# Decay tree on GpSimd, weight splits and the z projection moved inside a scan over heads, residuals read before the next split

## The chip, the cores and the metric

The kernel runs on 1 core of one Trainium2 chip. The metric is device time in microseconds. Three runs of the kernel before gave 2747.86 us as their median (2746.51 to 2750.76). The engines are called PE (TensorE, matrix products), DVE (VectorE), ACT (ScalarE), POOL (GpSimd) and SP (SyncE, which here only issues DMAs). Each runs its own instructions in order, and they meet through semaphores.

## The reference

Two blocks run one after the other on 512 tokens of width 1024, in float32. All products are float32-exact in effect, which the kernel reaches by splitting each operand into a high and a low part.

```
# first block, layer 0: gated linear recurrence (16 heads of 128, two directions, 256 context + 512 tokens)
p = (rms_norm(x) * (1 + scale) + shift) @ w_in          # five streams a head: q, f forward, f backward, v, z
q = silu(p[0]);  f = lb + (1 - lb) * sigmoid(p[1:3]);  k = 1 - f;  g = log(f)
S_t = diag(exp g_t) S_{t-1} + k_t v_t^T;   o_t = S_t^T q_t       # both directions, summed
y = rms_norm(o) * g_norm * silu(z);   x = x + gate * (y @ w_out)
# layer 1: 2-D Fourier mixer on 8 groups, then rms_norm(x, final_g)
# second block: 16 meta tokens in front, then
h = h + 0.5 * swiglu_ffn(rmsnorm(h))      # d_ff 2816
h = h + token_mixer(rmsnorm(h))           # causal convolutions, RG-LRU, gates
h = h + 0.5 * swiglu_ffn(rmsnorm(h));  out = rmsnorm(h)[16:]
```

## The kernel before

**Weights.** All weights come as one stream of 376 blocks of 128x1024 (512 KB), in two slots. For a block in slot `s`, SP loads `w_raw`; ACT copies it to `w_hi` (a rounded copy, `cut`, L812) once PE is done with the block that was in this slot; DVE computes `w_lo = w_raw - w_hi` (its own `cut`, L1265), which frees `w_raw` for the next load and releases PE. PE then runs three products for each 128x128 tile (`three`, L409): high by high, high by low, low by high. `after(k)` on ACT and DVE is the cut of block k+2, and on ACT it first waits until PE is done with block k. Where DVE or ACT has the cut in its queue decides what stands behind it.

**Heads.** Six blocks belong to one head: q, two f streams, v, z and a block for the modulation of a later layer. PE's loop (`pe_head(j + 1, j)`, 15 passes, one head in front and one behind outside the loop) projects head i = j+1 and between its parts does the scan of head j. Projections k go to PSUM bank `a = k % 2` (tokens) and bank `2 + k % 2` (context); ACT's `stage(k)` cuts a block, then reads the banks (`q_st`, `f_st`, `v_st`, `z_st`) and counts `acc_free` up, and PE's `free(k)` waits on that counter. The last two stages are z (k = 4) and the modulation (k = 5). After z is read, DVE's `prepare` makes `f_st`, `K`, `Q` and `ksum` of the new head and signals `gates_ready`. The banks 4 to 7 belong to the scan.

**The scan of a head** uses a tree of decays with 7 levels. At level l DVE's `merge(l)` does, in order: the product of neighbours `tree(l + 1)` from `tree(l)` (L1461; the leaves are `f_st`), growing `K` by the sibling's decay (L1469, then `k_grown`), growing `Q` (L1469), and placing PE's last scores into `ST` by a mask (L1446). ACT's `weave(l)` copies `K` into `K_now` (L932), and PE's `level(l)` multiplies `K_now` by `Q` (L568) once `weave(l)` and the growing of `Q` in `merge(l - 1)` are done. Then PE turns `K` (L581), makes the outer products (L590), DVE passes the states along (`passed`, L1487 and L1493), PE makes the output in bank 7 (L600 to L602), ACT squares it (`osq`, L937), PE sums the squares (`norm`, L609), ACT takes the root (`rt`, L942), and a head later DVE inverts it (L1504).

DVE's order in a head is: cut for stage 0, merges 0 to 2, cut for stage 1, merges 3 to 5, cut for stage 2, merge 6, the inversion, the states, the modulation, cut for stage 4, `prepare`, cut for stage 5. ACT's order at the end of a head is `stage(4)` (cut, `z_st`), square of the output, `stage(5)`, root. GpSimd issues DMAs only: in a loop over the heads it waits on `gate_used` and loads `gate_raw`, then `x1`, the Fourier tables, `meta` and at the end the output.

**Residuals.** `residual` and `raw_residual` add a finished product (nb blocks, PSUM) to a row of the stream. For each row m, DVE does all cuts of the nb blocks, then waits for the product, adds it (`stt`, L1592 or L1693), and where a norm follows, adds up the squares that ACT makes (L1303, L1308, or L1726 and L1727). The sums feed a matmul with `ones_d` (L445, L448) and a root on ACT.

**The first feed-forward** starts with unnormed rows and applies the rate afterwards. A pair of blocks (`one`: gate, up) ends in one row of `hid`. After the first pair PE also makes the mean for the final norm of the first block (L739). ACT has the root for it, `root(NFIN, ...)`, ahead of all pairs of the feed-forward; DVE inverts it in the second pair and applies it in the third and fourth.

Of the kernel before, what the change touches and what calls it, by code (L numbers as in the profile page):

```python
# [27 lines left out]
ALU = mybir.AluOpType  # L28
ACT = mybir.ActivationFunctionType
ds = bass.ds  # L30
# [20 lines left out]
RW = 4  # L51
EARLY = 4
EPS = 1e-6
LEVELS = 7
# [17 lines left out]

PER = {"head": 25 + 2 * (KD - 1), "mix": 74}

# [84 lines left out]
def program(nc, wts, ada_in, gate_in, x_in, ctx_in, meta_in, vec_in, mask_in, ident_in, dft_in, chan_in, out):  # L159
    nblocks = wts.shape[0]  # L160
    with ExitStack() as top:
# [135 lines left out]
        gates_ready = sem("gates_ready")  # L297
        k_grown, k_woven = sem("k_grown"), sem("k_woven")
        y_ready, y_hi_ready = sem("y_ready"), sem("y_hi_ready")
# [33 lines left out]
        def row(t, j):  # L333

            return t[:, j] if isinstance(j, int) else t[:, ds(j, 1)].rearrange("p a n -> p (a n)")

        def rate(j):
# [42 lines left out]
        @block.gpsimd  # L380
        def _(pool):
            pool.dma_start(xc[:], ctx_in).then_inc(xc_in_s, 16)
            pool.dma_start(masks[:], mask_in).then_inc(const_in_s, 16)
            pool.dma_start(ident[:], ident_in).then_inc(ident_in_s, 16)
            with pool.Fori(0, HEADS) as i:
                pool.wait_ge(gate_used, i + 1)
                pool.dma_start(gate_raw[:], gate_in[ds(i, 1)].rearrange("a p n -> p (a n)")
                               ).then_inc(gate_loaded, 16)
# [13 lines left out]
        def _(pe):  # L402
# [86 lines left out]
            def pe_head(i, j):  # L489
                def free(k):  # L490
                    pe.wait_ge(acc_free, i * 6 + (k + 1))

# [309 lines left out]
        def _(act):  # L802
# [70 lines left out]
            def act_head(i, j, f):  # L873
# [5 lines left out]

                def stage(k):  # L880

                    if i is None:
                        if j is not None and k < EARLY:
                            after(k)
                        return
                    if k == 3:
# [5 lines left out]
                    a, c = ps[:, k % 2], ps[:, 2 + k % 2]  # L892
# [226 lines left out]

            def feed_forward(tags, last_R, n, last, gated, product, hi):  # L1120
                c0 = TM - n
                for tag, count in zip(tags, FF_GROUPS):
                    S, before = ffn[tag]
                    with act.Fori(0, count) as i:
                        st.enter(i, 2)
                        after(0)
                        act.wait_ge(S["scaled"], i + (before + 2))
                        run(gated[:, 0:n], gated[:, 0:n], ACT.Silu).then_inc(S["gate"], 1)
                        after(1)
                        act.wait_ge(S["product"], i + (before + 1))  # L1130
                        run(row(hi, i)[:, c0:TM], product[:, 0:n], ACT.Copy).then_inc(S["hi"], 1)
                    st.leave(count)
                    final = tag == tags[-1]
# [3 lines left out]

            feed_forward(("f1a", "f1b", "f1c"), RD1, TM, False, sg1, hid1, hid1_hi)
            block_norm(NMIX)
# [107 lines left out]
            root(NF2, ps[:, 6], rate2[:, 0:T])  # L1247
            feed_forward(("f2a", "f2b", "f2c"), RD2, T, True, sg, hid, hid_hi)
            fetch_root()
# [5 lines left out]
        def _(dve):  # L1255
# [131 lines left out]

            def tree(l):

                if l == 0:  # L1390
                    return f_st[:]
                at = TA - (TA >> (l - 1))
                return f_tree[:, :, at:at + (TA >> l)]

            def dve_head(i, j, f):
# [57 lines left out]
                def merge(l):  # L1453


                    n = 2 ** l
                    prev = tree(l).rearrange("p d (m h) -> p d m h", h=2)
# [4 lines left out]
                    if l == 0:  # L1462
                        place(LEVELS, 4)
                    own.wait()

# [5 lines left out]
                    dve.wait_ge(k_woven, j * LEVELS + (l + 1))  # L1471
                    grow(K, 0, TA, 0).then_inc(k_grown, 1)
                    pe((3, 4, 6, 7, 8, 9, 10)[l])
                    if l:
# [5 lines left out]
                def passed(g_):  # L1480

                    pe((12, 14, 16)[g_])
                    whole_tile = tree(LEVELS)
                    acc = ps[:, 4 + g_ % 2].rearrange("p (x c) -> p x c", c=P)
# [37 lines left out]
                if j is None:  # L1522
# [54 lines left out]
            def residual(R, trips, nb, out_row, factor, n, sums, N=None, ahead=True, done=0):  # L1577
# [35 lines left out]
            for k in range(EARLY):  # L1613
                after(k)
                st.wait_done(dve, k)
                stt(x1[:, k], ps[:, k], gates[:, k, 0:1], x1[:, k], ALU.mult, ALU.add).then_inc(RC["res"], 1)
                add_square(RC, k, *sums)
            st.leave(1)
# [64 lines left out]
            def raw_residual(R, N, trips, nb, src, factor, gain, hi, lo, add):  # L1683


                with dve.Fori(0, trips) as i:
                    st.enter(i, 2 * nb)
                    for a in range(2):
                        for q in range(nb):
# [3 lines left out]
                        stt(src(m_), ps[:, 2 * a], factor(m_), src(m_), ALU.mult, ALU.add).then_inc(R["res"], 1)  # L1693
                        dve.wait_ge(N["hi"], m_ + 1)
                        stt(lo(m_), src(m_), gain(m_), hi(m_).bitcast(F32), ALU.mult, ALU.subtract
# [409 lines left out]
```

## Time and profile before

| | us |
|---|---|
| median of 3 runs | 2747.86 |
| lowest and highest | 2746.51 and 2750.76 |
| the profiled execution | 2748.82 |
| its span | 2747.2 |
| PE busy | 2564.4 (93% of the span) |
| DVE busy | 1625.9 (59%) |
| ACT busy | 1027.7 (37%) |
| POOL busy | 13.1 (28 DMA instructions) |
| mean granted clock of PE | 0.977 |

The span is that of the hardware profiler; the time of the execution also holds what lies around it. The heads take from about 55 to 997 us of the span, the Fourier mixer to 1350, its output product to 1447, the first feed-forward to 1842, the token mixer to 2352, the second feed-forward to the end.

In a timeline a row is: start in us from the span's start, length in us, engine, line, operation, output<-inputs, shape, count; the bracket at the end is the engine's idle time before it and what ended it. PE's records overlap each other (a 128x512 matmul is recorded at 0.40 us and the next one starts 0.23 us later), and so do DVE's by about 0.1 us, so distances between starts tell more than lengths. In a table of windows the columns are: the window, its length, then for PE, PEld, DVE, ACT and POOL the busy time and the count of instructions, then the granted clock of PE, the share of the DMA engines and GB/s. In a view by lines a row is: line, engine, operation, tiles, shapes, count, then busy us, mean ns of one, and idle time before them.

### The profile page before, as it was taken

To read this page: it belongs to the slowest core of one execution; us is meant where nothing else is said; L and a number is where in the kernel's file an instruction comes from. 1 tells how busy PE (TensorE), PEld (TensorE's weight loads), DVE (VectorE), ACT (ScalarE), POOL (GpSimd) and SP (SyncE) were. 2 spreads that over 40 slices of the span, in tenths; PEclk is the share of its full clock that TensorE was granted. 3 is DMA by queue.
4 is the path that set the end of the run, shared out by engine and by line. 5 is a ranking of instruction groups with operands and counts; after the bars stand their busy time and mean duration, and the time that the engine had idled before them with its cause. 6 is when DMAs were issued, how large, how long until landed. Compare 5 with 4: busy or idle time off the path is not lost.

```text
span 2747.2 us, 40135 instructions
## 1 busy us (share of the span) xinstructions
PE 2564.4 (93%) x14516; PEld 2191.1 (80%) x14516; DVE 1625.9 (59%) x2388; ACT 1027.7 (37%) x1349; POOL 13.1 (0%) x28
## 2 busy tenths in 40 slices
PE   6999999999999988999899999989999889999996
PEld 2788888888888775888688999988888757788885
DVE  5567777777777754333345443457999855534445
ACT  3334443444344323333234322235455533542222
POOL 0000000000000000000000000000000000000000
PEclk9999999999999998999899999999999999999998
DMA  5212211121112222222122222222222212222232
GB/s 219 69 62 76 70 61 61 62 83 61 61 53 89 79 85 69 69 69 69 45 94 74 91 87 92 92 92 85 89 87 91 85 54 88 89 99 92 92 99 84
DMA packets 59817, 224.34 MB, mean 82 GB/s; under 512 B 6496, under 2 KB 6496, under 8 KB 59136
## 3 DMA queue, kind: packets, MB, share of 16 engines
q1 hardware_dynamic: 56544, 207.94, 22.3%
q0 software_dynamic: 3232, 15.86, 1.5%
q8 instruction: 25, 0.41, 0.1%
q14 instruction: 16, 0.13, 0.0%
HBM read 221.68 MB, written 2.10 MB: 81 GB/s over the span
## 4 chain that ended last, share of the span: by engine, by line
PE 79%; DVE 9%; ACT 5%; issue 5%; DMA 1%; DVEq 0%; ACTq 0%; SPq 0%; POOL 0%
PE ps L409 71%; PE ps L568 3%; ACT w_hi L812 2%; PE ps L590 1%; DVE K L1469 1%; PE ps L466 1%; DVE w_lo L1265 1%; DVE cv L1826 1%; ACT K_now L932 1%; PE ps L581 1%; ACT L910 1%; DVE f_tree L1461 1%; DMA ada_raw<-in_ada_weights_dram 1%; PE ps L609 1%; DVE n_tmp L1826 0%
## 5 line engine op out<-in xcount | busy, mean ns | idle before, releaser
L1265 DVE TENSOR_TENSOR w_lo<-w_raw,w_hi 128x1024 fp32r<-128x1024 f32 x360 | 440.2, 1223 | 618.2 <-ACT w_hi L812 616.4
L812 ACT ACTIVATE w_hi<-w_raw 128x1024 fp32r<-128x1024 f32 x360 | 381.2, 1059 | 973.3 <-PE ps L409 939.5
L409 PE MATMUL ps<-n_hi,w_hi 128*128 128x512 f32 (+1 forms) x992 | 323.8, 358 | 29.7 <-DVE w_lo L1265 15.4
L409 PE MATMUL ps<-n_lo,w_hi 128*128 128x512 f32 (+1 forms) x992 | 320.2, 355 | 0.0
L409 PE MATMUL ps<-n_hi,w_lo 128*128 128x512 f32 (+1 forms) x992 | 319.8, 354 | 0.0
L409 PE MATMUL ps<-h_hi,w_hi 128*128 128x512 f32 x640 | 273.0, 427 | 9.2 <-DVE h_lo L1292 4.6
L409 PE MATMUL ps<-h_hi,w_lo 128*128 128x512 f32 x640 | 255.0, 398 | 0.0
L409 PE MATMUL ps<-h_lo,w_hi 128*128 128x512 f32 x640 | 254.8, 398 | 0.0
L409 PEld LDWEIGHTS ps<-n_hi,w_hi 128*128 128x128 f32 x992 | 175.4, 191 | 65.9 <-issue 20.2
L409 PEld LDWEIGHTS ps<-n_lo,w_hi 128*128 128x128 f32 x992 | 176.0, 190 | 26.7 <-issue 0.2
L409 PEld LDWEIGHTS ps<-n_hi,w_lo 128*128 128x128 f32 x992 | 175.8, 190 | 26.6
L568 PE MATMUL ps<-Q,K_now 128*128 128x128 f32 x896 | 129.4, 288 | 27.3 <-ACT K_now L932 25.8
L409 PEld LDWEIGHTS ps<-h_hi,w_hi 128*128 128x128 f32 x640 | 121.7, 190 | 39.3 <-issue 8.1
L568 PEld LDWEIGHTS ps<-Q,K_now 128*128 128x128 f32 x896 | 117.1, 191 | 44.3 <-ACT K_now L932 38.1
L409 PE MATMUL ps<-xg_hi,w_hi 128*128 128x264 f32 x704 | 144.8, 287 | 4.5 <-DVE w_lo L1265 4.5
L409 PEld LDWEIGHTS ps<-h_hi,w_lo 128*128 128x128 f32 x640 | 121.5, 190 | 29.2
L409 PE MATMUL ps<-xg_lo,w_hi 128*128 128x264 f32 x704 | 143.9, 287 | 0.0
L409 PE MATMUL ps<-xg_hi,w_lo 128*128 128x264 f32 x704 | 143.0, 284 | 0.0
L409 PEld LDWEIGHTS ps<-h_lo,w_hi 128*128 128x128 f32 x640 | 122.1, 191 | 24.2 <-issue 2.2
L409 PE MATMUL ps<-hid_hi,w_hi 128*128 128x264 f32 (+1 forms) x528 | 141.1, 321 | 0.0
L409 PE MATMUL ps<-hid_lo,w_hi 128*128 128x264 f32 (+1 forms) x528 | 141.0, 322 | 0.0
L409 PE MATMUL ps<-hid_hi,w_lo 128*128 128x264 f32 (+1 forms) x528 | 140.6, 320 | 0.0
(327 smaller groups left out, 5012.9 us busy)
## 6 DMA issues: line engine op xcount, KB each, us to landing
w_raw<-in_weights_dram SPq DMA_DIRECT2D x376, 512.0 KB, 3.3
ada_raw<-in_ada_weights_dram SPq DMA_DIRECT2D x4, 2048.0 KB, 25.2
gate_raw<-in_gate_weights_dram POOLq DMA_DIRECT2D x16, 512.0 KB, 4.8
x<-in_x_dram SPq DMA_DIRECT2D x1, 2048.0 KB, 9.3
x<-in_x_dram POOLq DMA_DIRECT2D x1, 2048.0 KB, 11.1
out_dram<-fin POOLq DMA_DIRECT2D x1, 2048.0 KB, 6.5
xc<-in_ctx_dram POOLq DMA_DIRECT2D x1, 1024.0 KB, 10.7
F_raw<-in_seq_dft_dram POOLq DMA_DIRECT2D x1, 1024.0 KB, 5.5
```

The costliest lines, as they stand in the source:

```text
L409: last = nc.tensor.matmul(o, w, xp, start=start and n == 0, stop=stop and n == 2)
L466: last = nc.tensor.matmul(ps[0:2, n], csil[:, k], raw_[:, :, k * P:(k + 1) * P], start=k == 0, stop=k == KD - 1)
L568: last = nc.tensor.matmul(ps[:, 5 - l % 2, tile(t)], K_now[:, l % 2, tile(t)], woven(Q, t * P, P, 2 ** l, 1), start=True, stop=True)
L581: last = nc.tensor.transpose(ps[:, 6, tile(x)], K[:, d, tile(ORDER[d][n])], ident[:])
L590: last = nc.tensor.matmul(ps[:, 4 + g_ % 2, tile(x)], KT[:, x], V[:, ORDER[d][n]], start=True, stop=True)
L609: nc.tensor.matmul(ps[:, 5], ones_h[:], osq[:], start=True, stop=True).then_inc(pe_scan, 1)
L812: run(w_hi[:, s], w_raw[:, s], ACT.Copy).then_inc(hi_ready[s], 1)
L910: run(z_st[:], a, ACT.Silu).then_inc(acc_free, 1)
L932: run(K_now[:, l % 2], woven(K, TC, T, 2 ** l, 0), ACT.Copy).then_inc(k_woven, 1)
L1265: tt(w_lo[:, s], w_raw[:, s], w_hi[:, s].bitcast(F32), ALU.subtract).then_inc(lo_ready[s], 1)
L1461: own.mark(tt(tree(l + 1), prev[:, :, :, 0], prev[:, :, :, 1], ALU.mult))
L1469: return tt(both(t, size, n, half), both(t, size, n, half), paired(*by, n), ALU.mult)
```

## The change

- The products of the decay tree leave DVE's `merge` and run on GpSimd, all seven of a head in a row after `gates_ready`, each waiting on the one before through a new semaphore `tree_grown`. GpSimd's load of `gate_raw` for the next head follows them. DVE's merges 1 to 6 and the passing of the states wait on `tree_grown`, and ACT waits for the first product before it writes `f_st` again.
- In a head's DVE order the cut for stage 0 moves behind merge 1, that for stage 1 behind merge 4, that for stage 2 behind merge 6. In `merge(0)` the placing of the diagonal goes behind the growing of `K`.
- z goes to PSUM bank 2 instead of bank 0, and projection 0 of the next head no longer waits for `z_st`. ACT cuts the block of stage 4, then squares the output, then reads z.
- In residuals the product is read right after it is done, ahead of the last cut instead of behind it.
- ACT takes the root of the final norm after the first pair of the first feed-forward.

```
+            pool.wait_ge(gate_used, 1)
+            pool.dma_start(gate_raw[:], gate_in[0:1]...).then_inc(gate_loaded, 16)
+            with pool.Fori(0, HEADS - 1) as i:
+                pool.wait_ge(gates_ready, i + 1)
+                for l in range(LEVELS):
+                    if l:
+                        pool.wait_ge(tree_grown, i * LEVELS + l)
+                    pair = siblings(l)
+                    nc.gpsimd.tensor_tensor(tree(l + 1), pair[:, :, :, 0], pair[:, :, :, 1], ALU.mult
+                                            ).then_inc(tree_grown, 1)
+                pool.wait_ge(gate_used, i + 2)
+                pool.dma_start(gate_raw[:], gate_in[ds(i + 1, 1)]...).then_inc(gate_loaded, 16)
...
     (PE)
-                    pe.wait_ge(acc_free, i * 6 + (k + 1))
+                    pe.wait_ge(acc_free, i * 6 + (k + (1 if k else 0)))
-                    a, c = k % 2, 2 + k % 2
+                    a, c = Z_BANK if k == 4 else k % 2, 2 + k % 2
...
     (ACT, a head)
                     elif k < 3:
                         if j is not None:
                             dve(1)
+                            act.wait_ge(tree_grown, j * LEVELS + 1)
...
                 cut_output()
+                refill(4)
+                squares_of_output()
                 stage(4)
-                squares_of_output()
                 stage(5)
...
     (DVE, a head)
-                    own.mark(tt(tree(l + 1), prev[:, :, :, 0], prev[:, :, :, 1], ALU.mult))
-                    if l == 0:
-                        place(LEVELS, 4)
-                    own.wait()
+                    else:
+                        dve.wait_ge(tree_grown, j * LEVELS + l)
...
                     grow(K, 0, TA, 0).then_inc(k_grown, 1)
+                    if l == 0:
+                        place(LEVELS, 4)
+                    own.wait()
...
-                next_block(0)
                 merge(0)
                 merge(1)
+                next_block(0)
                 merge(2)
-                next_block(1)
                 merge(3)
                 merge(4)
+                next_block(1)
                 merge(5)
+                merge(6)
                 next_block(2)
-                merge(6)
...
     (DVE, residual; raw_residual and the first four rows alike)
-                        for q in range(nb):
+                        for q in range(nb - 1):
                             if cuts:
                                 after(a * nb + q)
                         st.wait_done(dve, a * nb + nb - 1)
...
                         stt(r_, acc, factor(m_), r_, ALU.mult, ALU.add).then_inc(R["res"], 1)
+                        if cuts:
+                            after(a * nb + nb - 1)
                         if sums:
                             add_square(R, m_, *sums)
...
     (ACT, feed-forward)
-            root(NFIN, ps[:, 4], n1["sq"][:, 0])
+                    early = 0 if before else 1
+                    if early:
+                        one(S, 0, 0, 0)
+                        st.leave(1)
+                        aside()
...
+            feed_forward(("f1a", "f1b", "f1c"), RD1, TM, False, sg1, hid1, hid1_hi,
+                         lambda: root(NFIN, ps[:, 4], n1["sq"][:, 0]))
```

## Rows read from the trace of the kernel before

**Rows 1.** Windows: one pass of the heads' loop; the stretch after the third block's wait.

```profile
603.67:659.13 55.46, 53.02 (x323) 45.94 (x323) 40.71 (x70) 23.20 (x34) 0.53 (x1) 1.00 0.20 66
...
1461.50:1466.50 5.00, 4.99 (x23) 4.99 (x24) 3.05 (x4) 2.08 (x3) 0.00 (x0) 0.51 0.51 162
```

**Rows 2.** Timeline of PE, one pass of the heads' loop.

```profile
492.76 1.13 PE L609 MATMUL ps<-osq,ones_h 128*128 128x512 f32 x2 [0.66 <-ACT osq L937]
...
504.53 0.40 PE L409 MATMUL ps<-h_hi,w_lo 128*128 128x512 f32 x1
505.83 1.23 PE L568 MATMUL ps<-Q,K_now 128*128 128x128 f32 x8 [0.90 <-ACT K_now L932]
...
509.91 1.05 PE L568 MATMUL ps<-Q,K_now 128*128 128x128 f32 x8
...
518.28 1.16 PE L568 MATMUL ps<-Q,K_now 128*128 128x128 f32 x8 [0.79 <-ACT K_now L932]
...
529.28 0.40 PE L409 MATMUL ps<-h_hi,w_lo 128*128 128x512 f32 x1
529.77 0.65 PE L581 MATMUL ps<-ident,K 128*128 128x128 f32 x4
```

**Rows 3.** Timeline of DVE, the same pass.

```profile
492.59 1.27 DVE L1436 TENSOR_SCALAR f_st<-f_st,lbt 128x768 f32<-128x768 f32 x2 [0.47 <-ACT z_st L910]
...
495.91 0.68 DVE L1442 TENSOR_TENSOR ksum<-K 128x512 f32<-128x512 f32 x1
...
501.20 1.23 DVE L1265 TENSOR_TENSOR w_lo<-w_raw,w_hi 128x1024 fp32r<-128x1024 f32 x1 [3.47 <-ACT w_hi L812]
...
504.10 0.96 DVE L1469 TENSOR_TENSOR K<-K,f_st 128x768 f32<-128x768 f32 x1
...
528.68 0.96 DVE L1469 TENSOR_TENSOR K<-K,f_tree 128x768 f32<-128x768 f32 x1
```

**Rows 4.** Timeline of ACT, the same pass.

```profile
490.32 1.28 ACT L910 ACT_TABLE_LOAD   x1
491.62 0.60 ACT L910 ACTIVATE z_st<-ps 128x512 f32<-128x512 f32 x1
492.11 0.59 ACT L937 ACTIVATE osq<-ps 128x512 f32<-128x512 f32 x1
...
502.48 0.60 ACT L896 ACTIVATE q_st<-ps 128x512 f32<-128x512 f32 x1
...
516.79 0.38 ACT L901 ACTIVATE f_st<-ps 128x256 f32<-128x256 f32 x1
517.60 0.63 ACT L932 ACTIVATE K_now<-K 128x512 f32<-128x512 f32 x1 [0.43 <-DVE K L1469]
```

**Rows 5.** Timeline of PE, long waits outside the heads' loop.

```profile
104.44 0.79 PE L409 MATMUL ps<-h_hi,w_hi 128*128 128x512 f32 x1 [2.80 <-ACT z_st L910]
...
1066.74 2.08 PE L448 MATMUL ps<-n_sum,ones_d 128*128 128x512 f32 x2 [5.29 <-DVE n_sum L1308]
...
1447.72 1.16 PE L445 MATMUL ps<-both_sum,ones_d 128*128 128x264 f32 x4 [1.90 <-DVE both_sum L1727]
...
1461.51 0.80 PE L409 MATMUL ps<-xg_hi,w_hi 128*128 128x264 f32 x2 [4.48 <-DVE w_lo L1265]
...
2358.41 1.12 PE L448 MATMUL ps<-n_sum,ones_d 128*128 128x512 f32 x2 [1.28 <-DVE n_sum L1967]
```

**Rows 6.** DVE by lines: the tree's products, and the slowest elementwise group.

```profile
L1504 DVE RECIPROCAL rt<-rt 128x512 f32<-128x512 f32 x16 | 53.4, 3339 | 8.1 <-ACT rt L942 8.1
...
L1461 DVE TENSOR_TENSOR f_tree<-f_tree 128x384 f32<-128x384 f32 (+2 forms) x96 | 26.6, 277 | 0.0
...
L1461 DVE TENSOR_TENSOR f_tree<-f_st 128x768 f32<-128x768 f32 x16 | 15.2, 952 | 0.0
```

**Rows 7.** The page's DMA issues: size of one, us to landing.

```profile
gate_raw<-in_gate_weights_dram POOLq DMA_DIRECT2D x16, 512.0 KB, 4.8
```

**Rows 8.** Timeline of ACT at the final norm's root.

```profile
1457.07 0.69 ACT L826 ACTIVATE n_sq<-ps,eps 128x512 f32<-128x512 f32 x1 [7.45 <-PE ps L739]
```

**Rows 9.** Timeline of DVE, the last read of a product in a residual.

```profile
1063.80 0.74 DVE L1592 SCALAR_TENSOR_TENSOR x<-ps,gates,x 128x512 f32 x1
```

More of the change, by code:

```diff
@@ L52 @@
 EARLY = 4
+Z_BANK = 2
 EPS = 1e-6
@@ L69 @@
 NVEC = _at
-PER = {"head": 25 + 2 * (KD - 1), "mix": 74}
+PER = {"head": 18 + 2 * (KD - 1), "mix": 74}
 WIDE = (0, 1, 2, 3, 4, 5, 7, 8, 10, 11, 12, 13)
@@ L297, in program @@
         gates_ready = sem("gates_ready")
-        k_grown, k_woven = sem("k_grown"), sem("k_woven")
+        k_grown, k_woven, tree_grown = sem("k_grown"), sem("k_woven"), sem("tree_grown")
         y_ready, y_hi_ready = sem("y_ready"), sem("y_hi_ready")
@@ L335, in row, with tree, siblings @@
             return t[:, j] if isinstance(j, int) else t[:, ds(j, 1)].rearrange("p a n -> p (a n)")
+        def tree(l):
+            if l == 0:
+                return f_st[:]
+            at = TA - (TA >> (l - 1))
+            return f_tree[:, :, at:at + (TA >> l)]
+        def siblings(l):
+            return tree(l).rearrange("p d (m h) -> p d m h", h=2)
         def rate(j):
@@ L384, in _ @@
             pool.dma_start(ident[:], ident_in).then_inc(ident_in_s, 16)
-            with pool.Fori(0, HEADS) as i:
-                pool.wait_ge(gate_used, i + 1)
-                pool.dma_start(gate_raw[:], gate_in[ds(i, 1)].rearrange("a p n -> p (a n)")
-                               ).then_inc(gate_loaded, 16)
+            pool.wait_ge(gate_used, 1)
+            pool.dma_start(gate_raw[:], gate_in[0:1].rearrange("a p n -> p (a n)")).then_inc(gate_loaded, 16)
+            with pool.Fori(0, HEADS - 1) as i:
[7 more added lines that the diff above has]
+                pool.wait_ge(gate_used, i + 2)
+                pool.dma_start(gate_raw[:], gate_in[ds(i + 1, 1)].rearrange("a p n -> p (a n)")
+                               ).then_inc(gate_loaded, 16)
+            pool.wait_ge(gates_ready, HEADS)
+            for l in range(LEVELS):
+                if l:
+                    pool.wait_ge(tree_grown, (HEADS - 1) * LEVELS + l)
+                pair = siblings(l)
+                nc.gpsimd.tensor_tensor(tree(l + 1), pair[:, :, :, 0], pair[:, :, :, 1], ALU.mult
+                                        ).then_inc(tree_grown, 1)
             pool.wait_ge(w_used[1], 3 * HEADS + 1)
@@ L878, in dve, with refill @@
                     act.wait_ge(dve_scan, j * DVE_SCAN + n)
-                def stage(k):
+                def refill(k):
                     if i is None:
@@ L884, in stage @@
                             after(k)
-                        return
-                    if k == 3:
+                    elif k == 3:
                         s, _ = st.slot(5)
@@ L891, in stage @@
                         after(k)
-                    a, c = ps[:, k % 2], ps[:, 2 + k % 2]
+                def stage(k):
+                    if k != 4:
+                        refill(k)
+                    if i is None:
+                        return
+                    a, c = ps[:, Z_BANK if k == 4 else k % 2], ps[:, 2 + k % 2]
                     if k == 0:
@@ L1118, in block_norm, with feed_forward, one @@
                 norm_hi(N, lambda k: n_hi[:, k], lambda k: n2["tmp"][:, k % 2], lambda k: zero[:])
-            def feed_forward(tags, last_R, n, last, gated, product, hi):
+            def feed_forward(tags, last_R, n, last, gated, product, hi, aside):
                 c0 = TM - n
+                def one(S, j, before, passed):
+                    i = j + passed
+                    st.enter(j, 2)
+                    after(0)
+                    act.wait_ge(S["scaled"], i + (before + 2))
+                    run(gated[:, 0:n], gated[:, 0:n], ACT.Silu).then_inc(S["gate"], 1)
+                    after(1)
+                    act.wait_ge(S["product"], i + (before + 1))
+                    run(row(hi, i)[:, c0:TM], product[:, 0:n], ACT.Copy).then_inc(S["hi"], 1)
                 for tag, count in zip(tags, FF_GROUPS):
                     S, before = ffn[tag]
[L1124 to L1132, printed above, removed]
+                    early = 0 if before else 1
[3 more added lines that the diff above has]
+                        aside()
+                    with act.Fori(0, count - early) as i:
+                        one(S, i, before, early)
+                    st.leave(count - early)
                     final = tag == tags[-1]
@@ L1247, in _ @@
             root(NF2, ps[:, 6], rate2[:, 0:T])
-            feed_forward(("f2a", "f2b", "f2c"), RD2, T, True, sg, hid, hid_hi)
+            feed_forward(("f2a", "f2b", "f2c"), RD2, T, True, sg, hid, hid_hi, lambda: None)
             fetch_root()
@@ L1385, in _ @@
             dve.wait_ge(const_in_s, 16)
-            def tree(l):
-                if l == 0:
-                    return f_st[:]
-                at = TA - (TA >> (l - 1))
-                return f_tree[:, :, at:at + (TA >> l)]
             def dve_head(i, j, f):
@@ L1456, in merge @@
                     n = 2 ** l
-                    prev = tree(l).rearrange("p d (m h) -> p d m h", h=2)
+                    prev = siblings(l)
                     if l == 0:
@@ L1472, in merge @@
                     grow(K, 0, TA, 0).then_inc(k_grown, 1)
+                    if l == 0:
+                        place(LEVELS, 4)
+                    own.wait()
                     pe((3, 4, 6, 7, 8, 9, 10)[l])
@@ L1482, in passed @@
                     pe((12, 14, 16)[g_])
+                    if g_ == 0:
+                        dve.wait_ge(tree_grown, j * LEVELS + LEVELS)
                     whole_tile = tree(LEVELS)
@@ L1613, in _ @@
             for k in range(EARLY):
-                after(k)
                 st.wait_done(dve, k)
                 stt(x1[:, k], ps[:, k], gates[:, k, 0:1], x1[:, k], ALU.mult, ALU.add).then_inc(RC["res"], 1)
+                after(k)
                 add_square(RC, k, *sums)
@@ L1688, in raw_residual @@
                     for a in range(2):
-                        for q in range(nb):
+                        for q in range(nb - 1):
                             after(a * nb + q)
@@ L1693, in raw_residual @@
                         stt(src(m_), ps[:, 2 * a], factor(m_), src(m_), ALU.mult, ALU.add).then_inc(R["res"], 1)
+                        after(a * nb + nb - 1)
                         dve.wait_ge(N["hi"], m_ + 1)
```

2 lines of the change are left out of this document (removed).

## The prediction

> **What bounds the kernel now.** I read the table by stages first: one pass of the loop over the heads lasts 55.46 us at a granted clock of 1.00, with TensorE recorded busy for 53.02 us of it [rows 1]. There are 15 such passes (head i+1 is projected while head i is scanned) and they agree to 0.1 us, so a pass is worth reading closely. TensorE is the bound; what can be won is its idle time, and the time at half clock after a long one.
>
> The timeline of TensorE in one pass shows four stalls [rows 2]. The unstalled step from one 128x512 matmul to the next work is 0.23 us and an unstalled level is recorded at 1.05 us. Against that:
> - level 1 starts 1.30 us after the matmul before it instead of 0.23, and is recorded 0.18 longer: 1.25 us lost, on `K_now`;
> - level 4 sits idle 0.79 us, on `K_now`;
> - the first turn of `K` starts 0.49 us after the matmul before it: 0.26 us lost. The view names no releaser, but VectorE's last growing of `K` ends at 529.64 and the turn starts at 529.77 [rows 3], so it is that wait;
> - the matmul of the norm sits idle 0.66 us, on `osq`.
>
> Then VectorE and ScalarE in the same pass. VectorE stands idle for 3.47 us until the split `w_lo` of the next block can start at 501.20, does the split, the first product of the tree and a placing, and only at 504.10 grows `K` for level 0 [rows 3]. The growing does not need that split; it is only queued behind it. ScalarE has `q_st` done at 503.08, waits, and weaves late. For level 4 ScalarE has its second `f_st` done at 517.17 and weaves at 517.60 [rows 4]. And `osq` starts at 492.11, queued behind `z_st`, though the output is complete at about 491.8.
>
> Outside the heads the long waits of TensorE are single ones [rows 5].
>
> **The change, part by part, on the old clock.**
>
> *Heads, level 1.* In the new order `merge(0)` comes before the split, needs no tree (it reads `f_st`), and waits only for the diagonal, complete near 500.6. Growing `K` takes 0.96, so it ends at 501.6, not 505.06. ScalarE's `q_st` ends at 503.08 and the weave follows at about 503.0; a level starts 0.68 us after the start of its weave (517.60 to 518.28 [rows 2, 4]), so 503.7 against the 504.76 where TensorE can take it. The whole 1.25 us goes. What is late next is ScalarE, with 1 us to spare.
>
> *Level 4.* The split of `next_block(1)` moves behind `merge(4)`, so `merge(3)` ends early and the weave follows `f_st` at 517.18 instead of 517.60: 0.42 us gained. The rest of that stall stays, now on ScalarE's own queue (split, table load, two sigmoids).
>
> *First turn.* `merge(6)` goes ahead of the split that starts at 527.25 in the old order, so the last growing ends some 3 us sooner: 0.26 us gained.
>
> *osq before z_st.* `osq` at 491.80 instead of 492.11: 0.31 us gained. This is the part with a bill. The table load of 1.28 us that stood hidden ahead of `z_st` (490.32) now comes behind `osq`: load 492.35, `z_st` 493.65 instead of 491.62, 2.03 us later [rows 4]. VectorE's `prepare` waits for `z_st` (through the counter `acc_free`), so `f_st` moves from 492.59 to 494.6 and `ksum` from an end at 496.59 to 498.6 [rows 3]. Behind `prepare` on VectorE is the split that is needed by TensorE at 501.8; it ends at 499.8. The first weave moves from 498.03 to 498.7 and is needed after 500.3. Then VectorE is free at 499.8, before 500.6. All of it is covered by the 3.47 us of idle time above, so I cost it at nothing; without that cover it would be 2.03 us a head. The bank for z and the looser wait of projection 0 only keep TensorE from waiting for the later `z_st`.
>
> *The splits that come later.* Blocks 2, 3 and 4 are now split near 507, 519 and 526, and TensorE takes them near 513, 525 and 536; each split also frees the slot for SP's next load, whose block is used more than 10 us later. Nothing.
>
> *The tree on GpSimd.* It takes seven products a head off VectorE: 15.2 + 26.6 us in all, 2.6 a head [rows 6], none of it on a path once `merge(0)` is early. What GpSimd takes for them no row shows. The lower end is VectorE's own time, 0.95 us for the first and 0.55 for the second; the upper end is the slowest elementwise row, the reciprocal, 3339 ns for 512 elements, 6.5 ns each [rows 6]: 5.0 and 2.5 us. I take VectorE's rate, the same operation in the same shape. It starts at 498.7 and is first needed by `merge(1)` at 503.8, so with the engines independent even the upper end costs nothing. The load of `gate_raw` now waits on GpSimd's queue behind the seven products; it lands in 4.8 us [rows 7] and is read most of a head later.
>
> By the Trainium skill (GPSIMD Engine Reference, 3. Performance versus the Vector engine) a two-input product on GpSimd takes 1.96 times VectorE's time at 2048 elements, about 2.2 ns an element. As an estimate from that page the first two products take 1.7 and 0.85 us; the sum stays what it is, and no row here shows it.
>
> A head gains 1.25 + 0.42 + 0.26 + 0.31 = 2.24 us; 15 passes give 33.6. The last head has one more stall at level 1 (1.0 us). The start at 104.44 waits 2.80 us for `z_st`; the split it then waits for ends near 103.8: 0.65. Heads together: 35.2 us.
>
> *Final norm's root.* At 1457.07 ScalarE takes the root of the final norm after 7.45 us of waiting for the mean, and only then splits the third block [rows 8]; TensorE waits 4.48 us for it [rows 5], and then runs 5.0 us at a granted 0.51, the lower of its two clock levels [rows 1], which loses 2.4. With one pair of blocks ahead, ScalarE can split from about 1450.3 and VectorE, free of the reciprocal and the scaling, by 1455. Both go: 6.9 us. The root moves to a place where ScalarE is idle.
>
> *Residuals.* The read of the accumulator goes ahead of a split that it used to follow, in the shadow of ScalarE's half of that split. In the residuals with sums the add, the square and the closing add remain behind the split, so only the read's own time is saved, 0.66 (0.74 recorded, overlapped [rows 9]): at 1066.74 and at the like place at the end of the first feed-forward, 1.3 together. In `raw_residual` ScalarE's part starts as soon as its own split is done, so the sums are ready some 1.9 us sooner: the waits at 1447.72 (1.90) and 2358.41 (1.28) go [rows 5], 1.8 + 1.3. Elsewhere TensorE does not wait on this and nothing is gained. 4.4 us.
>
> Sum: 35.2 + 6.9 + 4.4 = 46.5 us. The profiled execution took 2748.8 us (span 2747.2); less 46.5 is 2702.3. The median shown is 1.0 below the profiled one, so 2701 to 2702: I say 2702.
>
> **Rivals.**
>
> *GpSimd and VectorE shut each other out (slower).* Mechanism: both read the same memory at the same time in each head near 499.8 to 504.4, and if one product on GpSimd holds VectorE for its whole length, growing `K`, then growing `Q` for level 1 queue behind the first two products. `Q` would end at 501.5 plus both their times, and is needed by 504.4: it decides from 2.9 us for the two together. At VectorE's rate (1.5) there is no stall. At the upper end (7.5) it is 4.6 us a head: 16 heads, +74 against -46.5, so 2776. Even with before at 5.8 us together. In between, about 2725. For it: 16 heads, tight place, nothing in the rows excludes it. Against it: it needs both the exclusion and a rate four times VectorE's.
>
> The Trainium skill (SBUF — State Buffer, Who interferes with whom) states this exclusion: a VectorE instruction with two SBUF inputs and a GpSimd instruction that reads SBUF block each other, whichever came first. By its rule with the other page's rate the two products take 2.55 us and 0.35 us is left, so still 2702. No row of before has GpSimd computing, so no row bears it out.
>
> *The later z_st becomes the bound.* If the chain `z_st`, `prepare`, first weave, split, `q_st`, second weave runs 2 us later than reckoned, level 1 waits as before, 16 times 1.25 us, and 26.5 of the 46.5 us stay: 2722. For it: the 2.03 us are real. Against: ScalarE's share of that chain was gated at 494.77 by a load anyway.
>
> *The heads give nothing* (each freed wait met by another of its length): only 11.3 us from outside, 2737. Against it: the stalls have named releasers that are plainly queued behind work they do not need.
>
> **How the numbers follow.** The forecast, 2696 to 2712: 0.68. Better than that, the rest of level 4 too: 0.04. Partial exclusion, 2712 to 2740: 0.12. Late z, 2716 to 2728: 0.07. Heads nothing, or no change: 0.03. Full exclusion, slower: 0.06. The range 2692 to 2722 leaves about 2 in 10 out. Faster by over 0.2% (5.5 us, about what a measurement of this kernel can tell): 0.91; within: 0.03; slower: 0.06.
>
> **What would show it.** A pass of 53.2 us; level 1 without idle time; level 4 idle 0.4 us behind `f_st`; the turn at 0.23 us behind its matmul; the norm idle 0.35; `z_st` about 2 us after `osq` with a load between. On GpSimd seven products a head starting with `ksum`'s end; growing `K` for level 0 right after the diagonal. If that growing starts later than 501, or its instructions are recorded longer than 0.96 us, the exclusion is real. Outside: no wait near 1461 and full clock there. Wrong would be a pass above 54.5 us.

## The result, and the profile after

| | before | after |
|---|---|---|
| median | 2749.31 (4 runs, 2746.51 to 2751.38) | 2705.33 (4 runs, 2701.14 to 2708.29) |
| the profiled execution, its span | 2748.82, 2747.2 | 2705.14, 2703.4 |
| ratio, 95% interval | | 0.9842, 0.9826 to 0.9857 |
| mean granted clock | 0.977 | 0.979 |

All times are in us. The change makes the kernel 44 us faster; 2702 was forecast, with a range of 2692 to 2722. The same kernel run again later as `e5_after_again` gave 2702.31, which is 47 less than the kernel before beside it. One of the four runs of e11, below, lasted 5107.89 and is left out of its figures.

The table of windows of the kernel after, for one pass of the heads' loop (against [rows 1]), and for the stretch of the first feed-forward in which the third block's wait and the half clock had been:

```profile
531.52:584.64 53.12, 52.54 (x322) 46.10 (x322) 39.04 (x62) 22.97 (x35) 7.01 (x8) 1.00 0.21 70
1403.00:1420.00 17.00, 16.97 (x119) 15.55 (x117) 10.12 (x10) 7.96 (x10) 0.00 (x0) 1.00 0.22 70
```

A pass is 53.12 instead of 55.46: 2.34 gained. TensorE's busy time is nearly the same (52.54 and 53.02), so it is idle time that went. GpSimd is now busy for 7.01 in a pass. In the feed-forward there is no gap and the clock stays at 1.00.

The timeline of TensorE, one pass, at the places of [rows 2]:

```profile
531.52 1.12 PE L636 MATMUL ps<-osq,ones_h 128*128 128x512 f32 x2 [0.34 <-ACT osq L971]
...
543.30 0.40 PE L436 MATMUL ps<-h_hi,w_lo 128*128 128x512 f32 x1
543.54 1.12 PE L595 MATMUL ps<-Q,K_now 128*128 128x128 f32 x8
...
555.34 1.16 PE L595 MATMUL ps<-Q,K_now 128*128 128x128 f32 x8 [0.24 <-ACT K_now L966]
...
566.33 0.39 PE L436 MATMUL ps<-h_hi,w_lo 128*128 128x512 f32 x1
566.56 0.60 PE L608 MATMUL ps<-ident,K 128*128 128x128 f32 x4
```

Level 1 starts 0.24 after the matmul before it, so its stall is gone. Level 4 idles 0.24 instead of 0.79, the turn of `K` follows at 0.23, and the norm idles 0.34 instead of 0.66.

The timelines of VectorE, ScalarE and GpSimd in the same pass, against [rows 3] and [rows 4]:

```profile
533.76 1.27 DVE L1474 TENSOR_SCALAR f_st<-f_st,lbt 128x768 f32<-128x768 f32 x2 [2.56 <-ACT z_st L944]
...
537.67 1.22 DVE L1310 TENSOR_TENSOR w_lo<-w_raw,w_hi 128x1024 fp32r<-128x1024 f32 x1
539.72 1.31 DVE L1505 TENSOR_TENSOR K<-K,f_st 128x768 f32<-128x768 f32 x1 [0.84 <-PE ps L582]
540.95 0.74 DVE L1484 COPY_PREDICATED ST<-masks,ps 128x512 f32<-128x512 int32 x1
541.82 1.03 DVE L1505 TENSOR_TENSOR Q<-Q,f_st 128x512 f32<-128x512 f32 x1
```

```profile
530.87 0.60 ACT L971 ACTIVATE osq<-ps 128x512 f32<-128x512 f32 x1 [1.48 <-PE ps L629]
531.49 1.28 ACT L944 ACT_TABLE_LOAD   x1
532.78 0.60 ACT L944 ACTIVATE z_st<-ps 128x512 f32<-128x512 f32 x1
...
541.41 0.60 ACT L929 ACTIVATE q_st<-ps 128x512 f32<-128x512 f32 x1
541.90 0.69 ACT L966 ACTIVATE K_now<-K 128x512 f32<-128x512 f32 x1
```

```profile
112.61 1.47 POOL L404 TENSOR_TENSOR f_tree<-f_st 128x768 f32<-128x768 f32 x1 [108.96 <-DVE ksum L1480]
114.15 3.76 POOL L404 TENSOR_TENSOR f_tree<-f_tree 128x384 f32<-128x384 f32 x6
...
537.84 2.38 POOL L404 TENSOR_TENSOR f_tree<-f_st 128x768 f32<-128x768 f32 x1 [45.19 <-DVE ksum L1480]
540.29 4.43 POOL L404 TENSOR_TENSOR f_tree<-f_tree 128x384 f32<-128x384 f32 x6
```

Three things are to be seen. `z_st` starts 1.91 after `osq` with the table load between them (1.85 by the forecast's own figures), and VectorE's idle time absorbs it. `K_now` for level 1 follows `q_st` at once, 541.90: ScalarE is the late one there, not VectorE. And GpSimd's first product takes 1.47 in the first head, where VectorE runs nothing beside it, but 2.38 in a pass, where the split `w_lo` runs at the same time. Growing `K` and `Q` on VectorE are recorded at 1.31 and 1.03, against 0.96 and 0.69 before.

Outside the heads, TensorE's waits that answer to [rows 5]:

```profile
105.90 0.49 PE L436 MATMUL ps<-h_hi,w_hi 128*128 128x512 f32 x1 [2.24 <-DVE w_lo L1310]
...
1032.38 1.22 PE L475 MATMUL ps<-n_sum,ones_d 128*128 128x512 f32 x1 [4.63 <-DVE n_sum L1353]
```

2.80 became 2.24 and 5.29 became 4.63. The waits of 1.90, 4.48 and 1.28 have no counterpart. The root of the final norm stands where ScalarE would be idle ([rows 8] before; the timeline of ScalarE after):

```profile
1421.65 1.28 ACT L853 ACT_TABLE_LOAD   x1
1422.94 0.69 ACT L853 ACTIVATE n_sq<-ps,eps 128x512 f32<-128x512 f32 x1
```

### The profile page after: what moved, and what is told of

Its sections match the earlier page's. It is cut to its first block, busy times and chain, and to the rows that moved or that the text cites. A ratio compares the mean times of both kernels' runs of the same rounds, so it can differ in the third digit from the quotient of the medians.

```text
span 2703.4 us, 40281 instructions
## 1 busy us (share of the span) xinstructions
PE 2556.3 (95%) x14516; PEld 2192.1 (81%) x14516; DVE 1602.4 (59%) x2276; ACT 1003.5 (37%) x1334; POOL 113.5 (4%) x140
## 4 chain that ended last, share of the span: by engine, by line
PE 85%; DVE 7%; ACT 4%; issue 3%; DMA 1%; DVEq 0%; ACTq 0%; SPq 0%; POOL 0%
PE ps L436 74%; PE ps L595 4%; PE ps L617 1%; PE ps L493 1%; DVE w_lo L1310 1%; DVE cv L1870 1%; ACT L934 1%; DMA ada_raw<-in_ada_weights_dram 1%; PE ps L636 1%; PE ps L608 1%; PE ps L627 1%; PE ps L582 1%; PE ps L629 1%; PE ps L628 1%; ACT w_hi L839 0%
```

## The experiments

The kernel before ran beside each group of kernels: 2750.86 beside e1 to e4, 2749.47 beside e5 to e8, 2749.24 beside e9 to e12 (7 runs each). Where a pass is given, it is the distance between two starts of the same matmul of TensorE.

**e1, the order without GpSimd.** The tree's products are back in VectorE's `merge`, and for level 0 the placing stands ahead of growing `K` again, as before; all else is the changed kernel. Of the edit, the product alone is shown.

```
-                nc.gpsimd.tensor_tensor(tree(l + 1), pair[:, :, :, 0], pair[:, :, :, 1], ALU.mult
+                    own.mark(tt(tree(l + 1), prev[:, :, :, 0], prev[:, :, :, 1], ALU.mult))
```

> The changed kernel with the decay tree back on VectorE, in its old place at the head of each merge (product, for level 0 the placing, then growing K); the new order of merges and splits stays. Theory, the order is enough: VectorE has room for the 2.6 us a head; in level 0 the product and the placing put the growing of K from 0.1 to 1.8 us behind the diagonal, the second weave then starts about 0.6 us later than in the changed kernel and level 1 about 0.3 us before TensorE wants it. So no stall comes back: a pass of 53.1 to 53.3 us, 2705 to 2709 us. Rival, the move to GpSimd is what pays: the growing for level 0 ends too late, level 1 waits about 1 us again, a pass above 54 us, 2720 us or more.

Measured: 2702.46 (2701.86 to 2702.66), ratio 0.9823 (0.9806 to 0.9839), a pass of 53.10.

```profile
487.02 0.96 DVE L1490 TENSOR_TENSOR K<-K,f_st 128x768 f32<-128x768 f32 x1
487.90 0.69 DVE L1490 TENSOR_TENSOR Q<-Q,f_st 128x512 f32<-128x512 f32 x1
...
500.97 1.16 PE L579 MATMUL ps<-Q,K_now 128*128 128x128 f32 x8 [0.24 <-ACT K_now L949]
```

With the tree on VectorE the changed kernel keeps its whole gain in the heads: given the new order, the place of the tree moves a pass by 0.02. The rival, a pass above 54, is out.

**e2, GpSimd without the order.** The splits are back at their old places, the tree stays on GpSimd, and the placing stays behind the growing of `K`.

```
+                next_block(0)
                 merge(0); merge(1)
-                next_block(0)
                 merge(2)
+                next_block(1)
                 merge(3); merge(4)
-                next_block(1)
                 merge(5)
+                next_block(2)
                 merge(6)
-                next_block(2)
```

> The changed kernel with the old order of merges and splits (split, merges 0 to 2, split, merges 3 to 5, split, merge 6); the tree stays on GpSimd and the placing behind the growing of K. Theory, either of the two parts alone removes the wait for K_now: the growing for level 0 is queued behind a split that can start about 0.4 us after the diagonal, but no longer behind a product and a placing; K_now for level 1 is in time and only the growing of Q for level 1 comes about 0.25 us late. A pass of 53.2 to 53.5 us, 2706 to 2712 us. Rival, the order is what pays: level 1 waits about 1 us and the first turn 0.3 us again, a pass of 54.4 us or more, 2724 us or more.

Measured: 2719.17 (2717.87 to 2722.52), ratio 0.9886 (0.987 to 0.9903), a pass of 54.33. That is between the two theories and nearer to the rival's 54.4. TensorE, then VectorE and GpSimd, from the timelines:

```profile
551.92 1.22 PE L595 MATMUL ps<-Q,K_now 128*128 128x128 f32 x8 [0.77 <-DVE Q L1505]
563.99 1.16 PE L595 MATMUL ps<-Q,K_now 128*128 128x128 f32 x8 [0.41 <-ACT K_now L966]
```

```profile
547.58 1.23 DVE L1310 TENSOR_TENSOR w_lo<-w_raw,w_hi 128x1024 fp32r<-128x1024 f32 x1 [1.24 <-ACT w_hi L839]
548.72 1.59 DVE L1505 TENSOR_TENSOR K<-K,f_st 128x768 f32<-128x768 f32 x1
...
545.29 2.37 POOL L404 TENSOR_TENSOR f_tree<-f_st 128x768 f32<-128x768 f32 x1 [45.73 <-DVE ksum L1480]
547.74 5.60 POOL L404 TENSOR_TENSOR f_tree<-f_tree 128x384 f32<-128x384 f32 x6
```

Level 1 waits for `Q`, and growing `K` is recorded at 1.59 where it was 0.96. A small product shows best what goes on. GpSimd's last one (128x12) takes 0.21 in the last head of this trace, where VectorE grows nothing beside it. In a pass it starts together with a growing of `K` and takes about as long as the two after each other:

```profile
552.30 1.04 POOL L404 TENSOR_TENSOR f_tree<-f_tree 128x12 f32<-128x12 f32 x1
552.32 0.95 DVE L1505 TENSOR_TENSOR K<-K,f_tree 128x768 f32<-128x768 f32 x1
```

The turn of `K` follows its matmul at 0.24 here too, so taking the tree off VectorE clears that stall as well as the new order does.

**e3, neither.** Both undone; `osq`, root and residuals stay changed.

> The changed kernel with both undone: tree on VectorE at the head of each merge, old order of merges and splits; the square ahead of z, the residuals and the final norm's root stay as changed. Theory: the stalls at level 1 (1.25 us), level 4 (0.4) and the first turn (0.26) come back, 1.9 us a pass, a pass of 55.0 us, 2733 to 2737 us. Rival, the later z with no cover left costs its own 2.0 us too: a pass of 57 us, 2765 us.

Measured: 2736.97 (2735.61 to 2738.75), ratio 0.9951 (0.9934 to 0.9967), a pass of 55.29; level 1 idles 1.06 and level 4 0.79. The time is as expected, the pass 0.3 longer. `osq` alone takes 0.32 off the norm's wait, but 0.16 of it comes back at level 1, whose idle time was 0.90.

**e4, z first.** `stage(4)` stands whole ahead of the square again.

```
                 refill(4)
-                squares_of_output()
                 stage(4)
+                squares_of_output()
```

> The changed kernel with z read ahead of the square of the output, as before; z stays in its new bank. Theory: the norm waits 0.31 us longer in each pass and nothing else moves, since prepare being 2 us earlier only adds to idle time of VectorE: a pass of 53.4 us, 2709 to 2711 us. Rival, the later z has a hidden price in the changed kernel (GpSimd and VectorE meet later, nearer to level 1): then this one is no slower, 2705 us or less.

Measured: 2706.67 (2705.91 to 2710.18), ratio 0.9841 (0.9825 to 0.9858), a pass of 53.44 with the norm idle for 0.66. In the pass it is the expected 0.32. The median is below the 2709 to 2711 expected. Its difference to the changed kernel (1.3, or 4.4 to e5) is no better known than the 3.0 between the two medians of one kernel, below.

**e5, the changed kernel again.**

> The changed kernel once more, for the pairs with the next runs. If the 0.2333 us pitch of its matmuls in the second feed-forward (0.2322 before, 1.5 us in all) belongs to the execution and not to the program, this run may show another value; if it belongs to the program, 0.2333 again. Time 2702 to 2706.

Measured: 2702.31 (2701.67 to 2703.01), ratio 0.9831 (0.9814 to 0.9847), a pass of 53.12. Its span is 2700.0 against 2703.4, and the two traces show where that lies. The timelines of TensorE in the second feed-forward, two matmuls that are 60 apart, in the first trace of the changed kernel and then in this one:

```profile
2322.79 0.40 PE L436 MATMUL ps<-n_lo,w_hi 128*128 128x512 f32 x1
...
2336.79 0.40 PE L436 MATMUL ps<-n_lo,w_hi 128*128 128x512 f32 x1
```

```profile
2321.52 0.39 PE L436 MATMUL ps<-n_hi,w_hi 128*128 128x512 f32 x1
...
2335.45 0.39 PE L436 MATMUL ps<-n_hi,w_hi 128*128 128x512 f32 x1
```

14.00 and 13.93, that is 0.2333 and 0.2322 a step, both at a granted clock of 1.00. From the norm ahead of that stage to the norm behind it the two take 369.33 and 367.75, 1.6 apart. The other stages agree, but for the start: the first matmul, which waits for a DMA, comes at 21.17 and at 19.97, and by the heads' loop the two are 1.49 apart. So the pitch belongs to the execution, not to the program. Over all fourteen traces of this record the stage takes either 369.3 (five of them) or 367.7 to 367.9 (nine).

**e6, the old order without GpSimd's work.** As e2, but GpSimd makes the tree of the first head alone and only raises the counter afterwards: the trees of heads 1 to 15 are left out.

```
             with pool.Fori(0, HEADS - 1) as i:
                 ...
+                pool.wait_ge(gates_ready, i + 2)
+                pool.sem_inc(tree_grown, LEVELS)
```

> The old order of the splits, as in the tree-only run, but GpSimd makes the tree of the first head alone; the trees of heads 1 to 15 are left out and the counter is raised without them. Theory (a product on GpSimd and one on VectorE exclude each other): growing K for level 0 is recorded 0.96 us again instead of 1.59, the stall at level 1 falls by about that to 0.2 or less, a pass lasts 53.7 us, 2710. Rival (the GpSimd work is independent and the 1.59 is the price of something else in the order): growing K stays at 1.59, pass 54.3, 2719.

Measured: 2708.55 (2708.25 to 2710.48), ratio 0.9854 (0.9838 to 0.9871), a pass of 53.68. The views by lines, growing `K` for level 0, of the changed kernel, of e1, e2 and e6:

```profile
L1505 DVE TENSOR_TENSOR K<-K,f_st 128x768 f32<-128x768 f32 x16 | 20.0, 1250 | 20.2 <-PE ps L582 20.2
```

```profile
L1490 DVE TENSOR_TENSOR K<-K,f_st 128x768 f32<-128x768 f32 x16 | 15.3, 959 | 2.0
```

```profile
L1505 DVE TENSOR_TENSOR K<-K,f_st 128x768 f32<-128x768 f32 x16 | 24.1, 1505 | 0.0
```

```profile
L1500 DVE TENSOR_TENSOR K<-K,f_st 128x768 f32<-128x768 f32 x16 | 15.5, 972 | 0.0
```

With the same program on VectorE, 1505 ns falls to 972 when GpSimd's products are not there, and the pass by 0.65. So it is GpSimd's products that lengthen VectorE's instructions, and the rival is out. That the two engines take turns, and do not merely slow each other, is what the pair of rows under e2 shows.

**e7, the root ahead of all pairs.**

```
             root(NF1, ps[:, 6:8, 0:HALF], halves(rate1[:]), eps_sq[:])
+            root(NFIN, ps[:, 4], n1["sq"][:, 0])
```

> The changed kernel with the root of the final norm back ahead of all pairs of the first feed-forward. Theory: the wait near the third block (4.5 us) and the half clock after it (2.4) come back: +6.9 us, so 2712. Rival (those stalls only moved, the first feed-forward gained through the residual ahead of it): +0 to 2, 2706.

Measured: 2706.70 (2705.49 to 2708.88), ratio 0.9849 (0.9832 to 0.9865); 4.4 above e5, and 3.55 in the stretch from the output product to the end of the feed-forward. Of the 6.9 expected half came. The wait (timeline) and the clock behind it (windows):

```profile
1421.23 0.50 PE L436 MATMUL ps<-xg_hi,w_hi 128*128 128x264 f32 x2 [3.06 <-DVE w_lo L1311]
```

```profile
1421.23:1426.23 5.00, 5.00 (x41) 5.00 (x42) 3.03 (x4) 2.05 (x3) 0.00 (x0) 1.00 0.52 151
```

The wait came back with 3.06 instead of 4.48, and the clock did not fall. ScalarE's split follows the root here directly, where before a table load of 1.28 stood between them; that is 1.28 of the 1.42. TensorE's wait was shorter, and it had not idled 1.90 some 13 us earlier, as it had before. Which of the two kept the clock up was not tested.

**e8, the old residuals.**

```
-                        for q in range(nb - 1):
+                        for q in range(nb):
...
                         stt(r_, acc, factor(m_), r_, ALU.mult, ALU.add).then_inc(R["res"], 1)
-                        if cuts:
-                            after(a * nb + nb - 1)
```

> The changed kernel with every residual's last read behind the last split again. Theory: the waits at the three places come back (1.9 at the output product, 1.3 at the start of the second feed-forward, 0.65 at two norms): +4.4 us, 2709.5. Rival (the later start of the following split ate the gain): +0 to 1, 2706.

Measured: 2706.59 (2704.98 to 2706.78), ratio 0.9844 (0.9827 to 0.986); 4.3 above e5, as expected, and 3.74 in the stretch from the output product to the end of the feed-forward.

```profile
1410.19 1.16 PE L472 MATMUL ps<-both_sum,ones_d 128*128 128x264 f32 x4 [1.88 <-DVE both_sum L1768]
...
2316.57 1.13 PE L475 MATMUL ps<-n_sum,ones_d 128*128 128x512 f32 x2 [1.28 <-DVE n_sum L2008]
```

```profile
1410.19:1415.19 5.00, 5.00 (x25) 4.87 (x26) 3.07 (x1) 1.96 (x3) 0.00 (x0) 0.66 0.00 0
```

The waits are back at the places named, and the two norms wait 5.29 and 5.39 again. Behind the first wait the clock is granted at 0.66 for 5 us, in which the changed kernel had full clock.

**e9 to e12, what is left.** e9 puts `weave(4)` ahead of `stage(1)` in ScalarE's order. e10 moves TensorE's norm of the finished head behind `project(0, "a")` of the next. e11 has both, and the residuals' add and sum ahead of the last split. e12 is e11 with the tree on VectorE.

```
(e9, ACT)                (e10, PE)
 weave(3)                -project(4, "b"); output(); project(5, "ada"); norm()
-stage(1)                +project(4, "b"); output(); project(5, "ada")
 weave(4)                -project(0, "a"); turn_v(range(CT, AT)); ...
+stage(1)                +project(0, "a"); norm(before); turn_v(range(CT, AT)); ...
```

> The changed kernel, with ScalarE's weave of level 4 ahead of stage 1 (split, table load, two sigmoids) instead of behind it. Theory (what is left of the stall at level 4 is ScalarE's own queue, and 0.24 to 0.5 us a pass are lost there with the late start of the next matmuls): level 4 without idle time, a pass of 52.8 us, 16 heads, -4 to -6 us: 2698. Rival (the freed time comes back because f_st, read later, holds up the projection's bank): level 4 free but a new wait at the projection behind it, 2702.

> The changed kernel, with TensorE's matmul of the norm (ones_h) for the finished head behind the first half of the next projection instead of right behind the output. Theory (its 0.34 us wait for osq and the slower start behind it are the last stall of a pass next to level 4's): no idle time ahead of it, a pass of 52.7 us, -5 to -7 us: 2697. Rival (the bank or the inversion that follows it becomes late): a new wait elsewhere in the pass, 53.1, 2702.

> The changed kernel with both of these, and in the residuals with sums the add and the square's sum ahead of the last split too (0.65 us or more at each of two norms). Theory: the three gains add, as they are stalls of one engine at different places: a pass of 52.4 us, 2689. Rival (taking away one stall exposes another of its length): 2697.

> The same with the tree's products back on VectorE. Theory (with the merges ahead of the splits the tree's place is of no matter): within 1.5 us of e11_all_free, 2688 to 2690. Rival (VectorE is now near the bound, and 2.6 us more a head are felt): 2693 or more.

| | median (range) | ratio (95%) | pass |
|---|---|---|---|
| e9 | 2692.77 (2692.14 to 2694.57) | 0.9796 (0.978 to 0.9812) | 52.61 |
| e10 | 2700.85 (2699.27 to 2701.64) | 0.9825 (0.9808 to 0.9841) | 52.92 |
| e11 | 2692.37 (2687.57 to 2692.38) | 0.9784 (0.9765 to 0.9804) | 52.41 |
| e12 | 2689.67 (2686.95 to 2693.65) | 0.9786 (0.977 to 0.9803) | 52.41 |

e9: the 0.24 at level 4 and the slower start behind it are gone, 0.51 a pass, 7.7 in 15 passes (4 to 6 were expected). Another 2.5 came in the last head, which took 53.94 from its first product to the next one's against 56.47 in e5, all of it by the clock. Windows over that last head, from e9, from e5 and from e11:

```profile
897.65:951.59 53.94, 45.58 (x244) 37.86 (x244) 37.90 (x49) 15.37 (x22) 5.37 (x8) 0.97 0.24 88
```

```profile
905.60:962.07 56.47, 48.11 (x243) 40.03 (x244) 37.75 (x48) 15.35 (x22) 5.36 (x8) 0.92 0.24 84
```

```profile
895.44:954.23 58.79, 50.43 (x245) 41.59 (x245) 37.93 (x48) 15.13 (x22) 5.35 (x8) 0.89 0.23 82
```

TensorE is idle for 8.36 in each of the three; only its busy time differs, for the same work at a mean clock of 0.97, 0.92 and 0.89.

e10: the norm no longer waits, but 0.15 of its 0.34 comes back on a split (timeline), so a pass gains 0.20, not 0.4; and ahead of the last head TensorE idles longer, 4.06 in e10 and 3.86 in e11 against 2.42 in e9. One row of e10, then two of e11:

```profile
528.44 0.50 PE L436 MATMUL ps<-h_hi,w_hi 128*128 128x512 f32 x1 [0.15 <-DVE w_lo L1315]
```

```profile
895.44 0.77 PE L436 MATMUL ps<-y_hi,w_hi 128*128 128x512 f32 x1 [3.86 <-ACT gates L952]
...
1020.12 1.25 PE L475 MATMUL ps<-n_sum,ones_d 128*128 128x512 f32 x2 [3.32 <-DVE n_sum L1358]
```

In the loop the gains add (0.51 + 0.20 = 0.71), and the sums ahead of the split take 1.31 off the norm's wait (4.63 to 3.32). The last head gives it back by the clock: 58.79 against 53.94 in e9. So e11 has the pass that was expected and not the time, 2692.37 for 2689. e9, e11 and e12 are faster than the changed kernel; for e10 that is not clear, and e9, e11 and e12 differ by less than their intervals. e12's expectation, that the tree's place does not matter, holds in the pass, 52.41 in both. The 2.7 between the medians is more than the 1.5 expected, but of the size that e5 showed for one kernel.

## Why the prediction was right, point by point

- **Level 1**: forecast 1.25, measured 1.17 (from the start of level 0 to that of level 2 it is 8.09 instead of 9.26). The stall is gone. ScalarE is next, as said.
- **Level 4**: forecast 0.42 gained and 0.40 left; measured 0.55 and 0.24. The forecast let the weave start where `f_st` is recorded to end (517.17). In the new order it starts 0.12 ahead of that end, as the rows of ScalarE overlap, and this is nearly all of the difference:

```profile
554.39 0.38 ACT L935 ACTIVATE f_st<-ps 128x256 f32<-128x256 f32 x1
554.65 0.63 ACT L966 ACTIVATE K_now<-K 128x512 f32<-128x512 f32 x1
```

That e2 and e6 idle 0.41 and 0.40 there is chance: in them `K` still grows behind the split, and its growing ends 0.12 ahead of the weave. e9 shows that what was left was ScalarE's own queue, as the prediction put it.
- **The turn** (0.26) and **`osq`** (0.31): 0.26 and 0.32, both as forecast. e3 shows that half of the latter is realised only when level 1 is free.
- **The bill of `osq`**: `z_st` was forecast 2.03 later. Against the last matmuls of the modulation (491.59 before, 530.67 after) it starts 2.08 later, hidden. The rival of the late z is out: `K_now` for level 1 starts at 541.90 and its level at 543.54, where 0.69 between the two is enough (554.65 and 555.34). So 1 us is to spare, as forecast. The new bank for z, which this part needs, was not undone by itself.
- **The tree on GpSimd**: the forecast took VectorE's rate, 0.95 and 0.55; alone they take 1.47 and 0.83 (the second in the last head). The premise that the engines are independent was wrong, and by the forecast's own sign, a growing recorded longer than 0.96, the mechanism of the slower rival is real (e2, e6). It cost nothing, because that rival's own condition decided: 2.9 us for the two products together, and they take 2.30. Growing `Q` ends at 542.85, 0.7 ahead of level 1. In the old order, where `merge(0)` has no slack, it costs 0.65 a pass. The Trainium skill (SBUF — State Buffer, Who interferes with whom) states this exclusion for a VectorE instruction with two SBUF inputs, and the traces agree: 1.47 alone and 2.38 beside a split. The Trainium skill's factor of 1.96 (GPSIMD Engine Reference, 3. Performance versus the Vector engine) is for an addition of 2048 elements; at 768 the runs show 1.47 against 0.95, 1.54.
- **A pass**: 2.24 forecast, 2.34 measured. The 15 passes gave 34.3 (33.6 forecast), not 15 times 2.34, mostly because the first pass lasted only 54.91 before; so they did not all agree to 0.1 as the forecast says. The first head gave 0.56 (0.65), the last one 0.86 (1.0). Together 35.7 against 35.2.
- **Root and residuals in the first feed-forward**: 6.9 + 1.8 + 0.66 = 9.4 forecast; that stretch took 493.15 before and takes 483.76, 9.39 less. The split of the sum was wrong: undone singly they cost 3.55 and 3.74 there (e7, e8), and 2.1 appear only with both old, as in the kernel before. The table load of 1.28 is one part of this. For the clock the runs show no simple rule: it fell behind the 4.48 of the kernel before and behind the 1.88 of e8, and not behind the 3.06 of e7.
- **The other residuals**: 0.66 and 1.3 forecast, 0.66 and 1.19 measured.
- **What no step held**: gains of 47.0 became 43.8 of span. 2.0 went at the start (the first matmul waits for a DMA until 21.17 instead of 19.70), 1.5 in the slower pitch, 1.1 by the clock in the token mixer (behind a wait of 7.45 in both traces it was granted at 0.70 for 5 us before, at 0.50 after). 0.9 came back at the end and 0.5 in the Fourier stage.

So 2702 was right for the reason given: stalls behind work that the waiting engine did not need. GpSimd had no part in it, as in the forecast's sum: e1, without it, is as fast. That the number agrees to 3 us is in part luck. The steps came out 0.5 above the 46.5 forecast, and the terms that no step held took 3.2 of it; e5 shows that two of them, the start and the pitch, differ between executions of one kernel.

## What to carry to other kernels

First look for instructions that stand in a queue ahead of work which does not need them; in this kernel the new order alone gave the loop's 34 us, and with it the move to another engine gave nothing. Before work goes to GpSimd beside a busy VectorE, add both engines' times at the place where something waits, as if they were one engine. Gains at two stalls that follow each other closely, here 14 us apart, need not be two independent terms: undo them one at a time, and both together.

## What the runs showed of the hardware

- GpSimd and VectorE took turns: a 128x768 product on GpSimd took 1.47 us alone and 2.38 beside a split of 1.22, a 128x12 product 0.21 alone and 1.04 beside a growing of 0.95; VectorE's growing took 0.96 alone, 1.31 or 1.59 beside GpSimd's products. The recorded length holds the time blocked.
- One program ran its 128x512 matmuls in one stage at 0.2333 us a step in one execution and 0.2322 in another, at full granted clock. In the other stages the two agree.
- After a wait of 1.88 the clock was granted at 0.66 for 5 us (e8), after one of 3.06 at 1.00 (e7): the length of the last wait alone did not tell. In the last head, the same work took 53.94 in e9, 56.47 in e5 and 58.79 in e11, with TensorE idle for 8.36 each time: the difference is the granted clock (0.97, 0.92, 0.89), and a single stage's gain of that size is not read from one trace.
